# Both low-rank products of the projection in high and low parts, with a split tile one column wider, and the recurrence's masks and first sums prepared inside attention

## The reference

```python
hn = rms_norm(x, attn_norm_g)
z = hn @ w_in                    # 3072 columns: dq, dk, dv, zr, zk, zv, 512 each
q, k = apply_rope(rms_norm(dq), ...), apply_rope(rms_norm(dk), ...)
o_diff = diff_attention(q, k, v, lam, ...)        # 4 heads, two maps each, causal
dh = token_shift(hn) - hn
xw, xa, xg = (hn + dh * mu_wag[m] for m in range(3))
w_log = -softplus(-(w0 + tanh(xw @ w1) @ w2)) - 0.5     # w1: 1024x64, w2: 64x512
a = sigmoid(a0 + (xa @ a1) @ a2)                        # 64 wide
g = sigmoid(xg @ g1) @ g2                               # 160 wide
o_rwkv = rwkv7_scan(r, decay, k, v, -kk, kk * a) ...    # 8 heads of 64, then norm, gate g
x = x + concat(o_diff, o_rwkv) @ w_out
```

## Time and profile before

| | |
|---|---|
| median of 3 runs | 3283.61 us |
| the profiled execution, its own time | 3288.2 us |
| its span, first to last instruction | 3286.5 us |
| PE busy | 2993.9 us (91%) |
| PEld busy | 2422.7 us (74%) |
| DVE busy | 2070.1 us (63%) |
| ACT busy | 1594.9 us (49%) |
| POOL busy | 794.2 us (24%) |
| mean granted clock of TensorE, share of 2.4 GHz | 0.960 |

### The profile page before, as it was taken

The page is one execution under the profiler, slowest core; times in us unless marked ns, Lnnn a source line. Parts: engine busy times, 40 slices in busy tenths (PEclk is TensorE's granted clock), DMA queues, the critical chain, the costliest instruction groups (busy, mean ns, idle before and its releaser), DMA issues. The chain is left out here.

```text
span 3286.5 us, 70126 instructions
## 1 busy us (share of the span) xinstructions
PE 2993.9 (91%) x25230; PEld 2422.7 (74%) x25230; DVE 2070.1 (63%) x3023; ACT 1594.9 (49%) x2597; POOL 794.2 (24%) x1075
## 2 busy tenths in 40 slices
PE   7999999997789894989988699989999999999799
PEld 5766887885566663877877588768888888887687
DVE  4343773223578774566666333369999999998575
ACT  2332211002677772444444211248888888887432
POOL 1000331000214125576676200011011010100353
PEclk9999999998899996999999799989999999999899
DMA  5554346556300001233233366565797867976663
GB/s 170 189 194 184 126 160 238 213 190 188 102 7 17 7 9 48 68 80 83 75 81 81 93 233 217 190 245 212 269 384 278 339 256 286 364 278 242 219 218 134
DMA packets 257102, 572.41 MB, mean 174 GB/s; under 512 B 35089, under 2 KB 71057, under 8 KB 248625
## 3 DMA queue, kind: packets, MB, share of 16 engines
q1 hardware_dynamic: 236192, 493.54, 43.2%
q0 software_dynamic: 11552, 41.95, 3.5%
q10 hardware_dynamic: 9072, 33.03, 2.5%
HBM read 417.96 MB, written 150.48 MB: 173 GB/s over the span
## 5 line engine op out<-in xcount | busy, mean ns | idle before, releaser
L583 PE MATMUL p_z<-w_in_part,hn_split 128*128 128x512 f32 x2304 | 535.5, 393 | 9.5 <-DMA hn_split<-s_hT 5.0
L583 PEld LDWEIGHTS p_z<-w_in_part,hn_split 128*128 128x128 f32 x2304 | 433.0, 189 | 100.1 <-DMA hn_split<-s_hT 5.9
L1769 DVE TENSOR_TENSOR e_w_part<-w_gate_up_sb,e_w_part 128x1024 fp32r<-128x1024 f32 x380 | 451.2, 1220 | 23.2 <-ACT e_w_part L1764 10.1
L1764 ACT CAST e_w_part<-w_gate_up_sb 128x1024 fp32r x380 | 398.1, 1052 | 120.7 <-PE pe_gate L2624 60.5
L2636 PE MATMUL pe_y<-e_w_part,e_hT 128*128 128x512 f32 x1128 | 271.2, 396 | 13.5 <-DVE e_w_part L1769 13.5
L2624 PE MATMUL pe_gate<-e_w_part,e_xT 128*128 128x512 f32 x1128 | 273.6, 399 | 7.0 <-DVE e_w_part L1769 7.0
L2624 PE MATMUL pe_up<-e_w_part,e_xT 128*128 128x512 f32 x1128 | 263.6, 389 | 0.0
L1769 DVE TENSOR_TENSOR e_w_part<-w_down_sb,e_w_part 128x1024 fp32r<-128x1024 f32 x188 | 217.9, 1220 | 59.5 <-ACT e_w_part L1764 59.2
L2636 PEld LDWEIGHTS pe_y<-e_w_part,e_hT 128*128 128x128 f32 x1128 | 210.4, 190 | 55.6 <-DVE e_w_part L1769 13.7
L2624 PEld LDWEIGHTS pe_gate<-e_w_part,e_xT 128*128 128x128 f32 x1128 | 211.3, 191 | 51.1 <-issue 7.6
L2624 PEld LDWEIGHTS pe_up<-e_w_part,e_xT 128*128 128x128 f32 x1128 | 211.8, 188 | 43.9
(11 more groups left out here) (439 smaller groups left out, 5717.0 us busy)
## 6 DMA issues: line engine op xcount, KB each, us to landing
w_gate_up_sb<-in_w_gate_dram SPq DMA_DIRECT2D x32, 2048.0 KB, 13.3
w_gate_up_sb<-in_w_up_dram SPq DMA_DIRECT2D x32, 2048.0 KB, 19.5
w_down_sb<-in_w_down_dram SPq DMA_DIRECT2D x32, 2048.0 KB, 9.2
hn_split<-s_hT SPq DMA_DIRECT2D x48, 1024.0 KB, 5.1
s_y<-e_y ACTq DMA_DIRECT2D x47, 512.0 KB, 6.0
...
s_zn<-z_stage SPq DMA_DIRECT2D x48, 256.0 KB, 2.0
```

The source lines that it names most:

```text
L583: last = nc.tensor.matmul(bank, hs[m % 3][:, a, k, :].bitcast(F32R), w_part(c, b)[:, k, :].bitcast(F32R), start=(k == 0 and a == b == 0), ...
L1764: return nc.scalar.copy(high, src)
L1769: return nc.vector.tensor_tensor(low, src, high, ALU.subtract)
```

## The change

1. lora_in becomes split products for tiles 1 to 15: 48 F32R products of 288 columns instead of 16 unsplit ones. Its stationary side is hn_split, made one column wider (129), so that it holds the shifted column too; lora_in now waits for h_low. Its weights are split once (lora_in_high on ScalarE, lora_in_low on VectorE in four pieces, after lora_in(0), which stays unsplit under the name lora_in_first). lora_in_high lies in slot 2 of the w_in chunks, so the split of the pieces 8 to 11 (chunk k) moves from tiles 10 to 13 to the end of the pass.
2. lora_out becomes 8 F32R products of 512 columns. The low parts of the 64 and 32 row products are packed beside their high parts in one 128-row product. lora_mid writes its results two or three times side by side, turn_l1 has four transposes, l1_turned on VectorE is replaced by l1_high_part (four copies on ScalarE) and l1_low_part (four subtractions on VectorE), and lora_midT has one buffer for two. The second weights are loaded by eight DMAs behind a wait for w_low and split once. The tables of angles share their memory, and are made after the pass.
3. In attention, the eight loads for the recurrence move from before the stores of o_stage to between them, at groups 32 to 39, with three of its parameters after; POOL makes the masks at the start and, after group 48, the first sums and the first kk0; VectorE makes the level masks. VectorE's wait for the parameters stands behind them.
4. The recurrence starts without masks: TensorE waits for cs_p only at step 0, ScalarE not at all; step -1 has three sums and one product less on POOL.

The core of the diff (declarations of semaphores, signatures, most of the moved mask code and the nesting of the phases are left out):

```diff
@@ -80,20 +80,34 @@
-        hs = [sb(f"hn_split{s}", [P, 2, KD, P]) for s in range(3)]
...
+        hs = [sb(f"hn_split{s}", [P, 2, KD, P + 1]) for s in range(3)]
...
+        wl_high = nc.alloc_sbuf_tensor_at("lora_in_high", [P, KD, 2, R_ALL], F32, offset=wl_at)
+        wl_low = nc.alloc_sbuf_tensor_at("lora_in_low", [P, KD, 2, R_ALL], F32, offset=wl_own)
+        wl_parts = [part[:].bitcast(F32R) for part in (wl_high, wl_low)]
...
+        l1T = sb("lora_midT", [P, 7, P])
@@ -135,7 +152,7 @@
-            for pass_, tile, first in ((0, 5, 4), (0, 10, 8), (1, 4, 12), (2, 1, 16), (2, 9, 20)):
+            for pass_, tile, first in ((0, 5, 4), (1, 4, 12), (2, 1, 16), (2, 9, 20)):
@@ -203,26 +220,29 @@
+            sp.wait_ge(w_low, W_PIECES)
+            for k in range(2):
+                sp.dma_start(w_raw_out[k * R_W:(k + 1) * R_W, :], t["w_lora_b"]).then_inc(s_lw, 16)
...
-                        sp.wait_ge(s_trig, 1)
+                        sp.wait_ge(lw_low, 1)
...
-                sp.dma_start(t["hT"][i * P:(i + 1) * P, :], hs[i % 3][:].rearrange("p a k n -> p (a k n)")).then_inc(stash[i % 3], 16)
+                sp.dma_start(t["hT"][i * P:(i + 1) * P, :].rearrange("p (a k n) -> p a k n", a=2, k=KD), hs[i % 3][:, :, :, 1:P + 1]).then_inc(stash[i % 3], 16)
@@ -313,14 +333,16 @@
-                nc.scalar.copy(hs[i % 3][:, 0, :, :].bitcast(F32R), hT[i % 2][:, :, 1:P + 1]).then_inc(h_high, 1)
+                nc.scalar.copy(hs[i % 3][:, 0, :, :].bitcast(F32R), hT[i % 2][:]).then_inc(h_high, 1)
...
-                nc.scalar.activation(l1[:, 0:R_W], pL[:, 0:R_W], ACT.Tanh)
-                nc.scalar.copy(l1[:, R_W:P], pL[:, R_W:P])
-                nc.scalar.activation(l1[:, P:R_ALL], pL[:, P:R_ALL], ACT.Sigmoid).then_inc(l1_act, 1)
+                act.wait_ge(ss_done, min(i + 2, TILES))
+                several = lambda a, n, c: (l1[:, a:a + n * c].rearrange("p (n c) -> p n c", n=n), [P, n, c])
+                for (out, shape), a, op in ((several(0, 2, R_W), 0, ACT.Tanh), (several(P, 2, R_A), R_W, ACT.Copy), (several(3 * P, 3, G1), 2 * P, ACT.Sigmoid)):
+                    nc.scalar.activation(out, pL[:, a:a + shape[2]].unsqueeze(1).broadcast_to(shape), op)
+                nc.scalar.activation(l1[:, 2 * P:3 * P], pL[:, P:2 * P], ACT.Sigmoid).then_inc(l1_act, 1)
@@ -336,6 +358,26 @@
+            def l1_high_part(i):
+                act.wait_ge(l1T_psum, i + 1)
...
+                    act.wait_ge(z_done, Z[("g", i - 1)] + 1)
+                nc.scalar.copy(l1T[:, 0:3, :].bitcast(F32R), pLT[:, 0:3 * P].rearrange("p (k n) -> p k n", k=3))
+                nc.scalar.copy(mid[5][0:R_W, :], pLT[0:R_W, 0:P])
+                nc.scalar.copy(mid[6][R_W:P, :], pLT[R_W:P, P:2 * P])
+                nc.scalar.copy(mid[3][0:3 * G1, :], pLT[0:3 * G1, 3 * P:4 * P]).then_inc(l1_high, 1)
@@ -345,21 +387,28 @@
+                if i == 0:
+                    act.wait_ge(s_wl_rdy, 1)
+                    nc.scalar.copy(wl_parts[0], wl[:]).then_inc(wl_h, 1)
...
+                l1_high_part(i)
+                if i == 0:
+                    split_out()
...
-                if i == 2:
-                    act.wait_ge(s_const, 1)
-                    act.wait_ge(s_ang, 1)
-                    nc.scalar.activation(sin_t[:], ang, ACT.Sin)
-                    act.wait_ge(s_ang, 2)
-                    nc.scalar.activation(cos_t[:], turns, ACT.Sin, bias=half_pi[:], scale=-1.0).then_inc(s_trig, 1)
...
+            for n in range(2 * W_PIECES, 3 * W_PIECES):
+                split(n)
+            act.wait_ge(s_const, 1)
+            act.wait_ge(s_ang, 1)
+            nc.scalar.activation(sin_t[:], ang, ACT.Sin)
+            act.wait_ge(s_ang, 2)
+            nc.scalar.activation(cos_t[:], turns, ACT.Sin, bias=half_pi[:], scale=-1.0).then_inc(s_trig, 1)
@@ -467,12 +516,20 @@
-            def l1_turned(i):
-                dve.wait_ge(l1T_psum, i + 1)
-                if i >= 2:
-                    dve.wait_ge(z_done, Z[("g", i - 2)] + 1)
-                nc.vector.tensor_copy(l1T[i % 2][:, 0:2, :], pLT[:, 0:2 * P].rearrange("p (k n) -> p k n", k=2))
-                nc.vector.tensor_copy(l1T[i % 2][0:R_G - P, 2, :], pLT[0:R_G - P, 2 * P:3 * P]).then_inc(l1T_sb, 1)
+            def l1_low_part(i):
+                dve.wait_ge(l1_high, i + 1)
+                nc.vector.tensor_tensor(mid[0][R_W:P, :], pLT[R_W:P, 0:P], mid[0][R_W:P, :], ALU.subtract)
+                nc.vector.tensor_tensor(mid[1][0:R_W, :], pLT[0:R_W, P:2 * P], mid[1][0:R_W, :], ALU.subtract)
+                nc.vector.tensor_tensor(mid[4], pLT[:, 2 * P:3 * P], mid[2], ALU.subtract)
+                nc.vector.tensor_tensor(mid[3][G1:2 * G1, :], pLT[G1:2 * G1, 3 * P:4 * P], mid[3][G1:2 * G1, :], ALU.subtract).then_inc(l1T_sb, 1)
+            def split_out():
+                dve.wait_ge(lw_high, 1)
+                nc.vector.tensor_tensor(wa_low[0:R_W, :], w_raw_out[0:R_W, :], w_rep[0:R_W, :], ALU.subtract)
+                nc.vector.tensor_tensor(wa_low[R_W:P, :], a_raw_out[R_W:P, :], a_rep[R_W:P, :], ALU.subtract)
+                nc.vector.tensor_tensor(g0_low, g0_raw, g0_high, ALU.subtract)
+                r = slice(2 * G1, 3 * G1)
+                nc.vector.tensor_tensor(g1_pack[r, :], g1_raw[r, :], g1_pack[r, :], ALU.subtract).then_inc(lw_low, 1)
@@ -490,20 +547,28 @@
+                if i == 0:
+                    dve.wait_ge(wl_h, 1)
+                    dve.wait_ge(l1_done, 1)
+                    for n in range(4):
+                        k = slice(n * KD // 4, (n + 1) * KD // 4)
+                        nc.vector.tensor_tensor(wl_parts[1][:, k], wl[:, k], wl_parts[0][:, k], ALU.subtract).then_inc(wl_l, 1)
...
-                l1_turned(i)
-                if i == 0:
-                    dve.wait_ge(s_out, 6 * 16)
...
+                l1_low_part(i)
+                if i == 0:
+                    split_out()
+                    dve.wait_ge(s_out, 2 * 16)
...
-                if i == 1:
-                    angles()
...
+            for n in range(2 * W_PIECES, 3 * W_PIECES):
+                split(n)
+            angles()
@@ -580,14 +645,26 @@
-                        last = nc.tensor.matmul(bank, hs[m % 3][:, a, k, :].bitcast(F32R), w_part(c, b)[:, k, :].bitcast(F32R),
+                        h = hs[m % 3][:, a, k, 1:P + 1] if p == 0 else hs_again[m % 3][:, a, k, :]
+                        last = nc.tensor.matmul(bank, h.bitcast(F32R), w_part(c, b)[:, k, :].bitcast(F32R),
...
+                pe.wait_ge(h_low, i + 1)
+                pe.wait_ge(l1_act, i)
+                for k in range(KD):
+                    if i == 1 and k % (KD // 4) == 0:
+                        pe.wait_ge(wl_l, k // (KD // 4) + 1)
+                    for shifted in (0, 1):
+                        for a, b in PARTS:
+                            last = nc.tensor.matmul(pL[:, 0:R_ALL], hs[i % 3][:, a, k, 1 - shifted:P + 1 - shifted].bitcast(F32R), wl_parts[b][:, k, shifted, :],
+                                                    start=(k == 0 and not shifted and a == b == 0), stop=(k == KD - 1 and shifted == 1 and a == 1))
+                last.then_inc(l1_done, 1)
+            def lora_in_first(i):
...
-                pe.wait_ge(l1_act, i)
@@ -597,18 +674,22 @@
-                nc.tensor.transpose(pLT[:, 0:P], l1[:, 0:P], ident[:])
-                nc.tensor.transpose(pLT[:, P:2 * P], l1[:, P:2 * P], ident[:])
-                nc.tensor.transpose(pLT[0:R_G - P, 2 * P:3 * P], l1[:, 2 * P:R_ALL], ident[:]).then_inc(l1T_psum, 1)
+                for k in range(3):
+                    nc.tensor.transpose(pLT[:, k * P:(k + 1) * P], l1[:, k * P:(k + 1) * P], ident[:])
+                nc.tensor.transpose(pLT[0:3 * G1, 3 * P:4 * P], l1[:, 3 * P:3 * P + 3 * G1], ident[:]).then_inc(l1T_psum, 1)
...
-                nc.tensor.matmul(bw, l1T[i % 2][0:R_W, 0, :], wab[0:R_W, :], start=True, stop=True).then_inc(z_done, 1)
-                nc.tensor.matmul(ba, l1T[i % 2][R_W:P, 0, :], wab[R_W:P, :], start=True, stop=True).then_inc(z_done, 1)
+                nc.tensor.matmul(bw, mid[0], w_rep, start=True, stop=False)
+                nc.tensor.matmul(bw, mid[5], wa_low, start=False, stop=True).then_inc(z_done, 1)
+                nc.tensor.matmul(ba, mid[1], a_rep, start=True, stop=False)
+                nc.tensor.matmul(ba, mid[6], wa_low, start=False, stop=True).then_inc(z_done, 1)
...
-                nc.tensor.matmul(bg, l1T[i % 2][:, 1, :], wg0[:], start=True, stop=False)
-                nc.tensor.matmul(bg, l1T[i % 2][0:R_G - P, 2, :], wg1[:], start=False, stop=True).then_inc(z_done, 1)
+                nc.tensor.matmul(bg, mid[2], g0_high, start=True, stop=False)
+                nc.tensor.matmul(bg, mid[2], g0_low, start=False, stop=False)
+                nc.tensor.matmul(bg, mid[4], g0_high, start=False, stop=False)
+                nc.tensor.matmul(bg, mid[3], g1_pack, start=False, stop=True).then_inc(z_done, 1)
@@ -621,10 +702,9 @@
-            lora_in(0)
+            lora_in_first(0)
```

(45 more changed lines are left out.)

163 lines of the change are left out of this document (100 added, 63 removed).

## The result

The changed kernel takes 3255.03 us (median of 5 runs, 3243.76 to 3261.18), against 3284.29 for the kernel before (5 runs). The ratio is 0.991, with a 95% interval from 0.9881 to 0.9939: 29 us faster. That is inside the range of the prediction (3222 to 3263), but 14 us short of the gain forecast, 42.9.

A forecast was written before the change was run, and what follows sets the result against it. TensorE, busy for 91% of the span, was taken to bound the kernel. Projection 21.8, attention 11 and recurrence start 10.1 us sum to 42.9 off the median 3283.6, given as 3241 us (range 3222 to 3263).

The forecast's parts named there:

- TensorE's side of the tile: First pass, per tile: lora_in 6.4 us, ending at c+8.8 (c: start of turn_l1); TensorE alone would need 15.1 us.
- (b): Weight loads pace the 288-column products at 0.188 us each: tile 17.7 us, kernel 3268 us; chance 0.05.
- (d): 288 columns too narrow for the fast form, two records of 246 ns per product: kernel 3475 us; chance 0.03.
- (a): TensorE in charge of first-pass tiles, the ScalarE work shorter than summed: 12 us more, kernel 3229 us; chance 0.10.
- ScalarE's chain: First-pass tile: added copies (0.9 us), square and hn put transposes at c+9.35; tile 15.7 us, 16.7 with weight split.
- the tile loop: First pass: thirteen tiles of 15.7 us and four extra us; c(15) at 285.5 for 306.86, gain 21.3 us.
- The start: First pass: lora_in(1) waits for hn's low part and the first quarter of lora_in_low; costs 4.8 us (2 to 7).
- the wait ahead of the transposes: First-pass tile: TensorE has lora_in done at c+8.8 and waits 0.6 us for transposes at c+9.35.
- The tables: Move to pass 1: Sin activations end near c+21.4, first k evacuated at c+24.1, so covered by 2.7 us.
- The wider split tile: First pass: hn_split one column wider, 1032 elements for 1024, 0.01 us, counted at nothing.
- Attention: First store no longer queued behind recurrence loads, 11.5 us; opening 0.5, 1 taken off: 11 us (4 to 13).
- Start of the recurrence: Cumulative product no longer waits for masks, one sum gone: first transposes +17.7 for +27.8, 10.1 us (7 to 13).

The follow-up runs named there:

- square_first: Changed kernel with ScalarE's square and VectorE's make_hn of tile i+2 ahead of l1_high_part(i) and l1_low_part(i) in pass 0; 3234.71 us, ratio 0.9835.
- the probe: Changed kernel with groups of 24 split products from different addresses put ahead of the projection; groups of 512 columns took 5.45 to 5.61 us.
- aligned: Changed kernel with the three hn_split buffers 8448 bytes apart instead of 8256, nothing computed differs; 3255.52 us, ratio 0.9894.
- before_spaced: Kernel before with a gap of 64 bytes behind each hn_split buffer, so they stand 8256 bytes apart; ratio 1.0034.
- head3_later: Changed kernel with attention's q, k, v loads of the fourth head issued behind the store of group 11; 3244.57 us, ratio 0.9874.

## Why the prediction was partly right

**TensorE's side of the tile** was right: 6.4 us for lora_in from records of a form that no row had (6.5), lora_in ended at c+8.8 as summed, and the tile that TensorE alone would need, 15.1, is `square_first`'s. Rivals (b) and (d), the slow narrow products, are out: 0.13 us each. So is (a), since TensorE waited for x_tile in every tile.

**ScalarE's chain** had the right mechanism and a term too small: l1_high_part takes 1.08 us (98.95 to the square's start at 100.03), estimated at 0.9, and it starts at c+4.7, not c+4.5. With a chunk of 5.69 instead of 5.57 (rows of 516 bytes, read from 4 bytes in; the probe has 5.59 for 5.45) the tile is 16.20 instead of 15.7: eight tiles, 4 us. Five tiles, not four, take 17.3 or more: the four with a weight split, where 16.7 was forecast, and the one ahead of them, where ScalarE's copy of g waits 1.2 us for the store of its buffer; what held that store was not tried. That is 4.1 us. Two of the five are longer still, 2.2 us in the first profile: one by a fall of the clock (1.5, last section), one by a further wait of that copy for a store (0.7). The sum is 10.3 us, nearly all of what the tile loop fell short (10.9 us gained between the first and the last turn_l1, 21.4 forecast). The start cost what was forecast: the first chunk stands 14.1 us behind the first turn_l1 (56.19 and 42.09), for 9.25 before (52.77 and 43.52), 4.85 for 4.8. The prediction had the wait ahead of the transposes in its sum at 0.6 us and called it small against the errors of eight offsets; it is the place where another order makes the kernel 23 us faster.

**The tables** were called covered by 2.7 us, and the first k came 1.3 us late. The step that failed is ScalarE's start behind pass 0: it was put at c+8.6, and it is c+11.6 (306.11), since the evacuation of g of the last tile waits for lora_out(15), which now waits for VectorE's low parts.

**The wider split tile** was costed at nothing, "0.01 us". That was its copies. What it does to every product that reads the buffers, in passes that the diff does not touch, was not asked: 5.3 us in passes 1 to 3 by `aligned`, 9 us in all four passes by `before_spaced`. This is the step that failed in kind and not in size.

**Attention**: 11 forecast, 8.9 and 10.5 measured. The store landed 7.3 us behind its issue instead of 6.3, the gap is 7.4 and not 6; the stall named there was the one, as `head3_later` shows. The GPSIMD Engine Reference of the Trainium skill (Specifications) has GpSimd share its SBUF interfaces with VectorE, with contention for VectorE instructions of two SBUF inputs, among others; what four GpSimd operations inside attention cost is lost in the spread of its length between profiles (466.4 to 471.2 us with them, 466.3 without).

**Start of the recurrence**: 10.1 forecast, 11.0 measured, +16.8 for +17.7, the mechanism as forecast.

**The sum** against the profile looked exact (3245 and 3243.8), and that was luck: 16 to 17 us too much in the projection, against 18.6 us by which stages that nothing edits were shorter in that one execution.
